# Expert stage: a large and a small expert share one pass, with their weight tiles in turn

## The chip, the cores and the metric

The kernel runs on one core of a Trainium2 chip. The metric is the device time of the program in microseconds (us), lower is better. Several runs of the kernel give a median; one further execution was recorded by the hardware profiler, and all rows below are from that one. Engines are named as in the profile: PE is the matmul engine (TensorE), PEld its weight loads, DVE is VectorE, ACT ScalarE, POOL GpSimd, SP the engine that issues the large loads.

## The reference, cut to what matters

A two-layer backbone in fp32 on 384 tokens (128 context, 256 latent). Layer 0 has an mLSTM and attention mixer and a dense SwiGLU, layer 1 a Mamba-2 mixer and then top-2-of-8 experts. The change touches the experts only, and the last residual and norm through what feeds them.

```python
D_MODEL = 1024; N_EXPERTS = 8; TOP_K = 2; D_FF_E = 1408

def swiglu(u, w1, w3, w2):
    return (jax.nn.silu(u @ w1) * (u @ w3)) @ w2

def moe_swiglu(u, router_w, router_b, w1, w3, w2):
    t = u.reshape(-1, d)                                  # 384 x 1024
    logits = (t @ router_w).astype(jnp.float32) + router_b.astype(jnp.float32)
    top_v, top_i = lax.top_k(logits, TOP_K)
    probs = jax.nn.softmax(top_v, axis=-1)
    gate = jnp.einsum('tk,tke->te', probs, jax.nn.one_hot(top_i, N_EXPERTS))
    for e in range(N_EXPERTS):
        out = out + gate[:, e:e + 1] * swiglu(t, w1[e], w3[e], w2[e])
```

## The kernel before

**Precision.** fp32 products are made of rounded parts. A weight tile (128 x 2816, 1408 KB) lands in one of four raw slots; ACT copies its high part into `whi` (`split`, L1235), DVE subtracts to get the low part `wlo` (`split`, L2247). There are three such pairs of buffers (`PAIRS = 3`), so ACT may split tile j only when PE has used tile j − 3 (`w_used`), and SP may load into a raw slot only when DVE has split what was in it (`split_lo`). `three` (L2934) makes hi·hi + hi·lo + lo·hi for 128 rows: three matmuls per block of 128 inputs. For 64 rows the high and the low part of the activations lie side by side in 128 columns ("packed"): two matmuls per block, with `whi` and `wlo`, and the two halves of the result's 128 lanes are then added (folded).

**Tiles.** An expert has 12 tiles: 8 up (tile 2f of `w1`, 2f + 1 of `w3`, 352 hidden columns each, f = 0 to 3) and 4 down (256 output columns each). A main up tile is 24 matmuls of 352 columns, a packed one 16; a main down tile is 33 matmuls of 256 columns, a packed one 22.

**Items.** The stage goes through a list of items; each is one pass over an expert's 12 tiles. Experts are ranked by their number of rows (expert 0 is apart and first). The three largest of the others have 128 main rows and 64 packed rows, the next has 128, the last three have 64. Rows beyond that go to further looped items.

| item | kind | what |
|---|---|---|
| 0 | main | expert 0; also ranks the experts and makes the item list |
| 1, 3, 5 | heavy (`heavy_item`) | ranks 0, 1, 2: 128 main and 64 packed rows on the same tiles |
| 2, 4 | light (`light_item`) | ranks 6, 5: 64 packed rows |
| 6 and on | main, in a hardware loop, at least one | rank 3, then rows left over |
| last | light, closing | rank 4: 64 packed rows |

**In an item.** PE takes the tiles in order; ACT applies silu from PSUM (L1275; packed L1311 copies the upper 64 lanes, L1316 is the silu), DVE makes the hidden product (`hidden`, L2413; packed `upper` L2431 and `packed_hidden` L2437 to L2439). After the last up tile PE transposes the hidden rows (`turn_h` L3366, `turn_packed` L3373), ACT and DVE split them, and the down tiles follow. Outputs are scaled by the gates when they leave PSUM (`out`, `packed_out` L1330 and L2454). ACT, DVE and POOL each have one queue in the program's order, so what waits holds back all behind it: `split` calls are written in between by hand.

**Rows of the next item.** DVE makes masks (`places`, `packed_places`), PE finds the row numbers with them (`find_rows` L3276, `packed_find` L3283), DVE turns them into indices (`next_rows`), POOL gathers the rows from `u_rows` in DRAM, PE transposes them in after the second down tile (`expert_in` L3292, `packed_in` L3299). POOL then adds the item's outputs to `y_rows` in DRAM (`scatter` L799, `packed_scatter` L808), each after the one before has landed (`y_added`). `rows_kept` (L2383) copies the indices for the scatter; in a looped item it waits for all scatters before.

**The end.** The closing item's outputs don't go through DRAM. POOL loads `y_rows` into `ytok` once the last scatter has landed, and `output_rows` (L3304, L3306) sums, for each of 8 blocks of 128 features, a matmul of `ye` with the one-hot `hotrow` (384 columns, two passes) and the transposed `ytok`. Four blocks go between the third and fourth down tile, four after it. The last residual and LayerNorm (`layer_norm`, `norm_steps`) follow.

Of the kernel before, what the change touches and what calls it, by code (L numbers as in the profile page):

```python
# [21 lines left out]
P = 128  # L22
# [24 lines left out]
ITEMS = NE + OVER  # L47
LAST = ITEMS - 1
# [3 lines left out]
Item = namedtuple("Item", "it m q h")  # L52
ITEM = (Item(0, 0, None, None), Item(1, 1, 0, 0), Item(2, None, 1, None), Item(3, 2, 2, 1), Item(4, None, 3, None),
        Item(5, 3, 4, 2))
LOOPED = len(ITEM)
RANKS = (0, 6, 1, 5, 2, 3, -1, -1, -1, -1, -1, 4)
ADDED = (0, 1, 4, 7)
PADDED = (2, 3, 5, 6, 8)


def looped(it):
    return Item(it, it - 2, None, None)


def closing(n):
    return Item(n, None, len(PADDED), None)


def next_main(x):

    if x.q == len(PADDED):
        return None
    if not isinstance(x.it, int) or x.it + 1 == LOOPED:
        return x.m + 1, x.it + 1
    return (ITEM[x.it + 1].m, x.it + 1) if ITEM[x.it + 1].m is not None else None


def next_packed(x):

    if not isinstance(x.it, int):  # L80
        return None
    if x.it + 1 == LOOPED:
        return len(PADDED), LAST, 0
    y = ITEM[x.it + 1]
    return (y.q, y.it, 0 if y.m is None else P) if y.q is not None else None


def added(m):
    return ADDED[m] if isinstance(m, int) and m < len(ADDED) else m + 5
# [7 lines left out]
for _n, _w in (("ident", 128), ("ropec", 128), ("ropes", 128),  # L97
               ("iota", 128), ("tri", 128), ("tie", 64), ("selp", 128), ("spread", 256), ("pm", 8), ("jrow", 16),
               ("erow", 8), ("rkrow", ITEMS - 1), ("caprow", 8), ("irow", OVER), ("tokc", 6), ("dummy", 2)):
    CI[_n] = (_at, _at + _w)  # L100
    _at += _w
# [40 lines left out]
def build(nc, i, o):  # L142
    ctx = ExitStack()
    with ctx:
# [243 lines left out]
        ye2 = rs.take(D, HALF)  # L388
# [6 lines left out]
        for _ in range(PAIRS):  # L395
# [4 lines left out]
        xp = rl.take(D).rearrange("p (k s) -> p k s", k=KB)  # L400
        heT2 = rl.take(FEB * P).rearrange("p (f s) -> p f s", f=FEB)
        rh = Region(arena[:, :], rl.at)
        he2, xrow2 = rh.take(FE, HALF), rh.take(D, HALF)
        fold2 = rh.take(2 * (FE // 4), HALF).rearrange("p (n w) -> p n w", n=2)
        part2 = he2[:, 0:D]
# [9 lines left out]
        ytok = [he[:, 0:D], spare[:, heT_at:heT_at + D], uT[:, :, :].rearrange("p a b -> p (a b)")[:, D:2 * D]]  # L415
        hotrow = he[:, D:D + T]
# [9 lines left out]
        gslot, gslot2 = re_.take(2), re_.take(3)  # L426
# [12 lines left out]
        hot, big2_ = (ro.take(OVER * 16) for _ in range(2))  # L439
        hotE, bigE = (ro.take((ITEMS - 1) * NE).rearrange("p (i e) -> p i e", i=ITEMS - 1) for _ in range(2))  # L440
        big = ro.take(C * (ITEMS - 1) * NE).rearrange("p (c i e) -> p c i e", c=C, i=ITEMS - 1)
        jover = ro.take(OVER)
        lists = sb("lists", [1, 16], I32)
        rows_in, rows_in2 = sb("rows_in", [P, 1], I32), sb("rows_in2", [P, 1], I32)
        rows_out, rows_out2 = sb("rows_out", [P, 1], I32), [sb(f"rows_out2_{n}", [P, 1], I32) for n in range(2)]
# [11 lines left out]
            "xp_lo": ("state_ready", 4), "packed_in_ready": ("num_ready", 2 * HA), "packed_out_ready": ("dspread_ready", 3),  # L457
# [56 lines left out]
        YBANK = (0, 1, 2, 3, 5, 0, 1, 2)  # L514
# [24 lines left out]

        def pbank(x, f, n):  # L540
            return ((5, 6), (4, 7))[f % 2][n] if x.h is not None else 2 * (f % 2) + n

        def obank(x, n):
            return (5, 6)[n] if x.h is not None else (7, 4)[n]
# [5 lines left out]
        def _(sp):  # L550
# [34 lines left out]
            def load_expert(e, s):  # L585
                sp.dma_start(slot(s % MRING), i["w_moe"][e, s] if isinstance(e, int) else
                             i["w_moe"][ds(e, 1), s].rearrange("a p n -> (a p) n")).then_inc(ready[s % MRING], 16)
# [3046 lines left out]
```

## Time and profile before

| | us |
|---|---|
| median of 3 runs | 1551.31 |
| lowest and highest run | 1545.7 and 1555.77 |
| profiled execution | 1554.25 |
| its span, first to last instruction | 1552.5 |
| PE busy in the span | 1418.6 |
| DVE busy | 1171.4 |
| ACT busy | 722.4 |
| expert stage to the end (996.8 to 1552.5) | 555.7 |

Busy time of PE counts each matmul from its start to its modelled end, and those overlap; the distance from one start to the next is what a matmul costs. Two engines can be busy at once, so busy times don't add up. Idle time of an engine matters only where PE or the end waits for it.

### The profile page before, as it was taken

The numbers are of one execution on the slowest core, as the hardware profiler recorded it, in microseconds if no ns is written. First come the engines' busy times: TensorE is split into PE (matmuls) and PEld (weight loads), VectorE is DVE, ScalarE is ACT, GpSimd is POOL, SyncE is SP. The second block draws the span as 40 slices with busy tenths as digits, with TensorE's granted clock in tenths as the row PEclk, the third lists the DMA queues.
The fourth block names the chain that finished last, engine by engine and source line by source line (L and its number), as shares of the span: only waits on it lengthen the run. The fifth ranks groups of instructions, "written<-read, shape, count | busy, mean of one in ns | idle before, by whom it ended". The sixth has DMA issues, their size and how long they took to land. (4 is left out here: it accounts for less than half of the span.)

```text
span 1552.5 us, 21728 instructions
## 1 busy us (share of the span) xinstructions
PE 1418.6 (91%) x8149; PEld 1273.2 (82%) x8149; DVE 1171.4 (75%) x1686; ACT 722.4 (47%) x1071; POOL 321.9 (21%) x409
## 2 busy tenths in 40 slices
PE   4999999799999997999999999889987997999966
PEld 1768876499999997998777698689987996999964
DVE  6868779768888796787778863787678659765885
ACT  1132223352333224644577742656466556656673
POOL 2201002720101003000699405300020001201103
PEclk9999999999999999999999899899999998999998
DMA  9525424445557541333322124478588759867871
GB/s 377 195 109 170 156 96 146 137 164 216 217 216 263 219 182 55 136 109 113 118 82 82 42 84 151 168 275 309 210 275 326 246 213 316 316 220 244 316 310 41
DMA packets 44718, 295.75 MB, mean 190 GB/s; under 512 B 5488, under 2 KB 5888, under 8 KB 21584
## 3 DMA queue, kind: packets, MB, share of 16 engines
q1 hardware_dynamic: 26496, 226.98, 39.7%
q0 software_dynamic: 17696, 65.94, 12.6%
q8 instruction: 60, 0.98, 0.3%
q10 hardware_dynamic: 432, 1.57, 0.3%
q14 instruction: 34, 0.28, 0.1%
HBM read 282.28 MB, written 12.19 MB: 190 GB/s over the span
## 5 line engine op out<-in xcount | busy, mean ns | idle before, releaser
L2247 DVE TENSOR_TENSOR arena_r<-arena,arena_r 128x2816 fp32r<-128x2816 f32 x96 | 295.2, 3086 | 95.1 <-ACT arena_r L1235 95.0
L1235 ACT ACTIVATE arena_r<-arena 128x2816 fp32r<-128x2816 f32 x96 | 244.9, 2553 | 92.1 <-PE ps L2937 68.8
L2937 PE MATMUL ps<-sqT_r,arena_r 128*128 128x384 f32 x963 | 261.0, 342 | 7.6 <-DVE uT_r L1896 7.6
L2937 PE MATMUL ps<-arena_r,uT_r 128*128 128x352 f32 (+2 forms) x636 | 204.5, 322 | 0.0
L2937 PEld LDWEIGHTS ps<-sqT_r,arena_r 128*128 128x128 f32 x963 | 178.4, 190 | 8.2 <-issue 8.2
L2937 PE MATMUL ps<-arena_r,zT_r 128*128 128x352 f32 x640 | 157.0, 328 | 7.1 <-DVE arena_r L2247 7.1
L2937 PE MATMUL ps<-arena_r,arena_r 128*128 128x384 f32 x848 | 159.9, 341 | 3.6 <-DVE zT L1907 2.4
L2937 PEld LDWEIGHTS ps<-arena_r,arena_r 128*128 128x128 f32 x848 | 150.0, 191 | 6.0 <-DVE zT L1907 2.7
L2937 PE MATMUL ps<-uT_r,arena_r 128*128 128x384 f32 x448 | 152.8, 341 | 0.0
L3334 PE MATMUL ps<-arena_r,arena_r 128*128 128x352 f32 x384 | 126.7, 332 | 17.1 <-DVE arena_r L2247 17.1
L3335 PE MATMUL ps<-arena_r,arena_r 128*128 128x352 f32 x384 | 124.5, 325 | 0.0
L2937 PEld LDWEIGHTS ps<-arena_r,uT_r 128*128 128x128 f32 x636 | 120.8, 190 | 4.4
L2937 PEld LDWEIGHTS ps<-arena_r,zT_r 128*128 128x128 f32 x640 | 113.1, 191 | 7.8 <-DVE arena_r L2247 7.7
L2700 PE MATMUL ps<-arena,uT 128*128 128x256 f32 x432 | 102.9, 393 | 0.3 <-DVE small L1762 0.3
L2700 PEld LDWEIGHTS ps<-arena,uT 128*128 128x128 f32 x432 | 82.4, 196 | 17.2 <-issue 5.5
L2937 PE MATMUL ps<-arena_r,spare_r 128*128 128x256 f32 (+1 forms) x504 | 96.1, 290 | 0.5 <-DVE arena_r L2247 0.5
L3334 PEld LDWEIGHTS ps<-arena_r,arena_r 128*128 128x128 f32 x384 | 73.5, 191 | 20.9 <-DVE arena_r L2247 19.6
L1881 DVE TENSOR_TENSOR arena_r<-arena,arena_r 128x2048 fp32r<-128x2048 f32 (+1 forms) x30 | 76.3, 2544 | 16.3 <-ACT arena_r L983 16.2
L2937 PEld LDWEIGHTS ps<-uT_r,arena_r 128*128 128x128 f32 x448 | 85.0, 190 | 0.0
L983 ACT ACTIVATE arena_r<-arena 128x2048 fp32r<-128x2048 f32 (+1 forms) x30 | 62.4, 2079 | 39.4 <-PE ps L2937 39.4
L2937 PEld LDWEIGHTS ps<-arena_r,spare_r 128*128 128x128 f32 x504 | 79.3, 189 | 1.0 <-DVE arena_r L2247 0.9
L3358 PE MATMUL ps<-arena_r,arena_r 128*128 128x256 f32 x264 | 70.9, 304 | 3.7 <-DVE arena_r L2445 3.6
(517 smaller groups left out, 2785.0 us busy)
## 6 DMA issues: line engine op xcount, KB each, us to landing
arena<-in_w_moe SPq DMA_DIRECT2D x96, 1408.0 KB, 6.5
arena<-in_w_up SPq DMA_DIRECT2D x22, 1024.0 KB, 5.8
zT<-in_w_adav POOLq DMA_DIRECT2D x32, 512.0 KB, 4.8
arena<-in_w_xbc SPq DMA_DIRECT2D x12, 1024.0 KB, 4.8
arena<-in_w_down SPq DMA_DIRECT2D x8, 1408.0 KB, 6.6
spare<-in_w_adav POOLq DMA_DIRECT2D x20, 512.0 KB, 5.2
sqT<-in_w_adav POOLq DMA_DIRECT2D x16, 512.0 KB, 3.7
arena<-in_w_z SPq DMA_DIRECT2D x8, 1024.0 KB, 4.8
```

The costliest lines, as they stand in the source:

```text
L983: nc.scalar.activation(fwhi[n % 2][:, 0:width], slot(g % RING)[:, 0:width], ACT.Copy) \
L1235: nc.scalar.activation(whi[s % PAIRS], slot(s % MRING), ACT.Copy) \
L1881: V.tensor_tensor(slot_r(g % RING)[:, 0:width], slot(g % RING)[:, 0:width], fwhi[n % 2][:, 0:width].bitcast(F32), ALU.subtract).then_inc(S ...
L2247: V.tensor_tensor(wlo[s % PAIRS], slot(s % MRING), whi[s % PAIRS].bitcast(F32), ALU.subtract) \
L2700: m = M.matmul(ps[:, bank + c, 0:256], uT[:, k, c * P:(c + 1) * P], slot(g % RING)[:, k * 256:(k + 1) * 256], start=k == 0, stop=k == KB - 1)
L2937: m = M.matmul(out, a, b, start=first and n == 0, stop=last and n == 2)
L3334: M.matmul(ps[:, pbank(x, f, n), 0:W], xp[:, k, :], whi[s % PAIRS][:, w], start=k == 0, stop=False)
L3335: e = M.matmul(ps[:, pbank(x, f, n), 0:W], xp[:, k, :], wlo[s % PAIRS][:, w], start=False, stop=k == KB - 1)
L3358: M.matmul(out, heT2[:, f, :], whi[s % PAIRS][:, w], start=f == 0, stop=False)
```

## The change

Heavy and light items disappear. A large expert and a small one now form a pair item of 24 tiles, one of each in turn (even tiles the large one, odd tiles the small one). Each even tile has 24 main and 16 packed matmuls, each odd one 16. The packed rows of both ("halves") share the 128 lanes of the folded values: the large expert's 64 rows in the lower lanes, the small one's in the upper. So there is one silu, one product and one set of transposes for both; the fold stays one per half and tile.

| item | kind | what |
|---|---|---|
| 0 | main | expert 0 |
| pair 0, 1 | pair | ranks 0 and 6, ranks 1 and 5 |
| looped, at least one | main | rank 3, then rows left over |
| closing pair | pair | ranks 2 and 4: 256 rows in the last pass |

Further: the halves' gate is multiplied into the hidden product, not onto the output. The main rows of a pair have PSUM banks 0 and 1 only (before 0 to 3). `xrow2`, the landing place of the next pair's gathered half rows, lies in `he2`, so its gather waits for the transposes of `he2`. POOL scatters the main rows, then half 0, then half 1, each after the one before has landed. `rows_kept` waits for main scatters only, and in a looped item it stands after split 6 instead of split 4. `ytok` lies in `xp` and a raw slot, so its loads wait until the closing pair has used its 16 up tiles and split 21 tiles (before: until the item ahead was done). `output_rows` has a second one-hot matmul, for the halves.

```diff
-ITEM = (Item(0, 0, None, None), Item(1, 1, 0, 0), Item(2, None, 1, None), Item(3, 2, 2, 1), Item(4, None, 3, None),
-        Item(5, 3, 4, 2))
-RANKS = (0, 6, 1, 5, 2, 3, -1, -1, -1, -1, -1, 4)
+PAIR_COLS = ((1, 2), (3, 4), (12, 13))
+ITEM = (Item(0, 0, None), Item(1, 1, 0), Item(3, 2, 1))
+RANKS = (0, 6, 1, 5, 3, -1, -1, -1, -1, -1, -1, 2, 4)
...
-        he2, xrow2 = rh.take(FE, HALF), rh.take(D, HALF)
+        he2 = Region(arena[:, :], rl.at).take(FE)
+        xrow2 = he2[:, 0:D]
...
+            def half_gather(h):
+                gp.wait_ge(*since("packed_in_ready", h + 1))
+                if h:
+                    gp.wait_ge(*since("phT_mm", h * 3))
...
-            gp.wait_ge(S("y_added"), n_last * 16 + 64)
-            gp.wait_ge(S("w_used"), n_last * MOE_TILES)
+            gp.wait_ge(S("y_added"), m_last * 16 + 16)
+            gp.wait_ge(*since("y_half", 64))
+            gp.wait_ge(S("split_lo"), n_last * MOE_TILES + 21)
+            gp.wait_ge(S("w_used"), n_last * MOE_TILES + 16)
...
+            def halves_hidden(x, f):
+
+                v.wait_ge(*since("psilu_ready", x.h * 4 + f + 1))
+                V.scalar_tensor_tensor(he2[:, f * (FE // 4):(f + 1) * (FE // 4)], fold2[:, 0, :],
+                                       gslot2[:, x.h:x.h + 1], fold2[:, 1, :], ALU.mult, ALU.mult) \
...
             def output_rows(b):
 
                 M.matmul(ps[:, YBANK[b], 0:T], ye[:, b * P:(b + 1) * P], hotrow, start=True, stop=False)
+                M.matmul(ps[:, YBANK[b], 0:T], ye2[:, b * P:(b + 1) * P], hotrow2, start=False, stop=False)
...
```

The three queues of a pair item, as the new code has them (ACT and DVE: first the first three groups of four tiles, then what follows; j is the tile):

```diff
+            def pair_item(x):                      # DVE
+                for f in range(3):
+                    fold(x, 0, f, 0)
+                    split(it, 4 * f + 3)
+                    fold(x, 1, f, 0)
+                    split(it, 4 * f + 4)
+                    hidden(x, f)
+                    fold(x, 0, f, 1)
+                    split(it, 4 * f + 5)
+                    fold(x, 1, f, 1)
+                    halves_hidden(x, f)
+                    split(it, 4 * f + 6)
+                    if f == 1:
+                        if last:
+                            rows_kept(x.m)
+                        else:
+                            next_rows(x)
...
+            def pair_item(x):                      # PE
+                for s in range(8):
+                    split_done(x, 2 * s)
+                    up_main(x, s, 2 * s)
+                    up_half(x, 0, s)
+                    split_done(x, 2 * s + 1)
+                    up_half(x, 1, s)
+                    if s == 1 and not last:
+                        next_found(x)
+                    elif s == 6:
+                        turn_h(x, 0, 2)
+                        turn_h(x, 1, 3)
+                turn_h(x, 2, 4)
+                turn_halves(x, 0, 2)
+                turn_halves(x, 1, 3)
+                for n in range(4):
+                    split_done(x, 16 + 2 * n)
+                    down_main(x, n, 16 + 2 * n)
+                    if n == 0:
+                        turn_halves(x, 2, 4)
+                    down_half(x, 0, n)
+                    if n == 1 and not last:
+                        halves_in(next_pair(x), (0, 3))
+                    elif n == 2 and not last:
+                        expert_in(next_main(x)[0], (0, 3))
+                    elif n == 2:
+                        for b in range(4):
+                            output_rows(b)
+                        first_mean(3)
+                    split_done(x, 17 + 2 * n)
+                    down_half(x, 1, n)
```

ACT in a group: `silu`, `lower(0)`, split 4f + 3, `lower(1)`, split 4f + 4, `halves_silu`, `lower(0)`, split 4f + 5, `lower(1)`, split 4f + 6. In the closing pair the last two folds of the outputs stand in DVE's queue behind the fourth block of the last residual.

## Rows read from the trace of the kernel before

**Rows 1.** Windows by item: stretch, its length, busy (count), PE clock, DMA share, GB/s

```profile
996.80:1057.70 60.90, 54.19 (x372) 52.83 (x371) 53.62 (x73) 37.36 (x25) 3.87 (x2) 0.97 0.79 291
1057.70:1194.20 136.50, 121.68 (x834) 118.94 (x832) 97.53 (x94) 82.22 (x71) 11.29 (x6) 0.96 0.76 270
1194.20:1329.80 135.60, 121.91 (x832) 119.17 (x832) 98.91 (x95) 80.84 (x70) 11.66 (x6) 0.96 0.76 271
1139.80:1194.20 54.40, 40.28 (x258) 38.27 (x256) 45.04 (x47) 39.80 (x33) 8.42 (x4) 0.91 0.90 319
1329.80:1413.50 83.70, 83.01 (x590) 82.24 (x591) 56.31 (x58) 42.33 (x39) 8.46 (x3) 1.00 0.67 239
1413.50:1470.00 56.50, 51.60 (x351) 50.83 (x350) 40.73 (x31) 35.69 (x23) 6.96 (x3) 0.97 0.82 305
1470.00:1524.50 54.50, 42.46 (x263) 38.60 (x261) 44.54 (x41) 33.91 (x30) 5.28 (x6) 0.94 0.65 252
1524.50:1552.50 28.00, 12.55 (x49) 8.19 (x48) 15.71 (x30) 10.47 (x19) 13.32 (x13) 0.79 0.15 56
1470.00:1498.40 28.40, 22.25 (x130) 20.26 (x128) 26.18 (x19) 22.07 (x18) 3.42 (x4) 1.00 1.00 381
```

Busy times stand in the order PE, PEld, DVE, ACT, POOL. The stretches are item 0, items 1 and 2, items 3 and 4, item 2 alone, item 5, the looped item, the closing item, the tail, and the up tiles of the closing item.

**Rows 2.** Order of time on PE, heavy items: start, us, what

```profile
1057.72 0.32 PE L3334 MATMUL ps<-arena_r,arena_r 128*128 128x352 f32 x1
...
1060.29 0.49 PE L2937 MATMUL ps<-arena_r,zT_r 128*128 128x352 f32 x2
...
1111.31 1.42 PE L3366 MATMUL ps<-cons,spare 128*128 128x128 f32 x11
...
1343.28 0.82 PE L3283 MATMUL ps<-spare,zT 128*128 128x16 f32 x6
```

**Rows 3.** Chain of waits in order of time, heavy item 3

```profile
1197.02 3.84 PE ps L2937 x24
...
1252.13 3.93 PE ps L2937 x33
```

**Rows 4.** Order of time on PE, light item 2, behind its last up tile

```profile
1175.72 1.44 PE L3373 MATMUL ps<-cons,arena 64*128 64x64 f32 x11 [5.47 <-DVE arena L2439]
```

**Rows 5.** Groups of heavy item 1 (busy us, mean ns, idle before), then of the stage

```profile
L2247 DVE TENSOR_TENSOR arena_r<-arena,arena_r 128x2816 fp32r<-128x2816 f32 x13 | 40.2, 3092 | 26.7 <-ACT arena_r L1235 26.7
L1235 ACT ACTIVATE arena_r<-arena 128x2816 fp32r<-128x2816 f32 x12 | 30.6, 2554 | 15.5 <-PE ps L2937 15.5
L1311 ACT ACTIVATE arena<-ps 64x352 f32<-64x352 f32 x8 | 3.7, 462 | 0.7 <-PE ps L3335 0.6
L2437 DVE TENSOR_TENSOR arena<-ps,arena 64x352 f32<-64x352 f32 x4 | 2.0, 511 | 0.0
...
L2454 DVE SCALAR_TENSOR_TENSOR sqT<-ps,spare,arena 64x512 f32<-64x512 f32 x10 | 7.4, 735 | 0.0
```

**Rows 6.** Chain of waits, looped item: the packed scatter of item 5

```profile
1422.53 11.18 DMA y_rows<-sqT,rows_out
```

**Rows 7.** Order of time on PE, looped item

```profile
1438.07 0.87 PE L2937 MATMUL ps<-arena_r,zT_r 128*128 128x352 f32 x2 [4.39 <-DVE arena_r L2247]
```

**Rows 8.** Order of time on PE, output blocks of the closing item

```profile
1515.81 0.81 PE L3304 MATMUL ps<-spare,sqT 128*128 128x384 f32 x2
1516.46 0.61 PE L3306 MATMUL ps<-cons,spare 128*128 128x128 f32 x4
...
1517.13 0.81 PE L3304 MATMUL ps<-spare,sqT 128*128 128x384 f32 x2
...
1526.99 1.65 PE L3304 MATMUL ps<-spare,sqT 128*128 128x384 f32 x2 [2.48 <-ACT sqT L1338]
```

**Rows 9.** DMA issues of the whole span: count, KB each, us to landing

```profile
arena<-in_w_moe SPq DMA_DIRECT2D x96, 1408.0 KB, 6.5
```

**Rows 10.** DMA issues from 1020 us on: count, us to landing

```profile
spare<-y_rows POOLq DMA_DIRECT2D x2, 512.0 KB, 11.7
...
arena<-u_rows,rows_in POOLq DMA_INDIRECT x6, 10.5
```

More of the change, by code:

```diff
@@ L1255, in rows_stored, with expert_in @@
                 act.dma_start(u_dram[c * P:(c + 1) * P, :], utok[:, c, :]).then_inc(S("u_stored"), 16)
-            def expert_in(m, halves=range(2), bank=0):
+            def expert_in(m, halves=range(2), banks=(0, 1)):
                 for n in halves:
@@ L1397, in light_item @@
[L1397 to L1412 removed]
+                    lower(x, 0, f, 0)
@@ new lines, in pair_item @@
+                split(it, 16)
+                halves_silu(x, 3)
+                lower(x, 0, 3, 1)
+                split(it, 17)
+                lower(x, 1, 3, 1)
+                hidden_hi(x, 2)
+                halves_hi(x, 0)
+                halves_hi(x, 1)
+                split(it, 18)
+                halves_hi(x, 2)
+                split(it, 19)
+                split(it, 20)
+                out(x, 0)
+                lower_out(x, 0, 0)
+                split(it, 21)
+                if not last:
+                    halves_in(next_pair(x), (0, 3))
@@ new lines, in next_rows, with output_slots @@
+                if next_pair(x) is not None:
+                    v.wait_ge(*since("found2_mm", next_pair(x) + 1))
+                slot_rows(*next_main(x))
+                if next_pair(x) is not None:
+                    half_rows(next_pair(x))
+            def inputs(x):
+                expert_in_lo(next_main(x)[0])
+                if next_pair(x) is not None:
+                    halves_in_lo(next_pair(x), (2, 3))
+            def output_slots(dst, row):
+                for c in range(C):
+                    step(V.tensor_scalar(rowc[:, c:c + 1], row, con("dummy")[:, 0:1], float(-P * c), ALU.add, ALU.add))
+                    V.tensor_scalar(dst[:, c * P:(c + 1) * P], con("iota"), rowc[:, c:c + 1], None,
+                                    ALU.is_equal).then_inc(S("hot_ready"), 1)
@@ L2506, in main_item @@
                 split(it, 6)
+                if not opening:
+                    next_rows(x)
                 split(it, 7)
@@ L3418, in main_item @@
                 for s in range(6):
+                    if s == 1 and not opening:
+                        pe.wait_ge(*since("ye2_ready", 2 * 4 - 1))
                     split_done(x, s)
-                    up_main(x, s)
+                    up_main(x, s, s)
                     if s == 0 and opening:
```

795 lines of the change are left out of this document (362 added, 433 removed).

## Prediction

> **What bounds the kernel now.** I read the windows by item first, then TensorE's order of time inside one heavy item, then the idle time in the light ones, then VectorE and ScalarE by group, and last the DMA. Only the expert stage is touched, 996.8 to 1552.5 us, so everything ahead of it is taken as unchanged.
>
> The windows [rows 1] show three kinds of item. A heavy item (a large expert's 128 rows plus 64 packed rows on the same weight tiles) keeps TensorE busy: item 5 has 83.0 busy of 83.7 us, at a granted clock of 1.00. A light item (64 packed rows alone) has TensorE busy 40.3 of 54.4 us, at 0.91. So the light items are held by something else, while the heavy ones are held by TensorE and leave VectorE and the DMA slack. A heavy-light couple takes 136.5 and 135.6 us.
>
> What TensorE needs follows from the starts of its matmuls [rows 2]. The 16 packed matmuls of a 352-column tile begin at 1057.72 and the next group at 1060.29: 2.57 us, 0.160 each. The chain of waits gives 3.84 for the 24 of the main rows and 3.93 for 33 of 256 columns [rows 3], so 22 packed ones of 256 columns take 2.62. Eleven 128-row transposes cost 1.4, one find of rows about 0.7 (0.82 less its overlap) [rows 2].
>
> In a light item an up tile is 2.57 us of TensorE, but VectorE needs 3.09 for its split (the low part of the weight tile) and 0.5 for each fold [rows 5], and at the turn from up to down nothing is left to multiply: TensorE waited 5.47 us for the last hidden product [rows 4]. The light item's clock of 0.91 [rows 1] adds to that.
>
> **The change, part by part.** Tiles stay 96 and the experts' row capacities stay (192 for the three largest, 128 for the next, 64 for three), so matmuls on weights stay equal in number. What changes is what stands beside what.
>
> *Pairs 0 and 1 take the place of two heavy-light couples.* TensorE per pair: up, 8 × (3.84 + 2 × 2.57) = 71.8; two finds 1.4; transposes of hidden values, 11 for the main rows and 11 for both halves together (before 11 + 11 + 11), 2.8; down, 4 × (3.93 + 2 × 2.62) = 36.7; 16 input transposes at 1.4/11 each, 2.0. Sum 114.7. Two of these are 229.4 against 272.1 [rows 1]: −42.7, if TensorE never waits.
>
> Does it wait? Take one group of four up tiles, 2 × (3.84 + 5.14) = 17.96 us of TensorE. VectorE has four splits (12.4), four folds (4 × 0.51), the main product (as a fold, 0.51) and one product for both halves (taken at 0.55 between 0.51 for the same columns and 0.74 for the 512-column scalar-tensor form, since it is now 352 columns with the gate as third operand): 15.5 [rows 5], or 86%. ScalarE has four splits at 2.55, four lower halves at 0.46 and two silus, taken at 0.5: 13.0 [rows 5]. A split of tile j+3 may begin when tile j is used (three split pairs). Counting from the group's start: tile 0 is used at 6.4; ScalarE copies the lower half (6.9), splits tile 3 (9.5), VectorE ends it at 12.6; it is wanted at 15.4. Tile 4 goes 12.5 on ScalarE and 16.2 on VectorE (a fold ahead of it); wanted at 17.96. The main product, now needed before the next main tile because the main rows have only banks 0 and 1, comes at 16.7: margin 1.3. Tiles 5 and 6 end at 21.5 and 25.6, wanted at 24.4 and 26.9. So every hand-off has 1.3 to 2.9 us. The next items' row numbers (some 2.2 us of one-column VectorE work, placed after the second group) eat one such margin.
>
> At the turn the transposes of blocks 0 to 7 of the main rows now lie between tiles 13 and 14, and the main down matmuls stand ahead of the halves' last transposes. The last hidden product of the halves comes about 2 us after tile 15, while TensorE has 1.4 us of transposes and 3.9 of main matmuls to do. The 5.47 wait has cover. Without it, it would come back at about 2 to 3 us a pair.
>
> The gate in the inner product removes the scaling at the output, where a scaled copy on ScalarE and a scaled add on VectorE (0.74 [rows 5]) become a plain copy and add. Outputs of halves double in number against items, not against experts: nothing, hidden under 9.2 us of TensorE per down step.
>
> *New waits.* The gather of the next pair's 128 half rows uses the space of the hidden values, so POOL may issue it only when the last halves' transposes are done, about 12 us before TensorE wants the rows. Gathers landed 10.5 us after issue in the median [rows 10]. Late, TensorE itself stands there with the next down tile behind it. I allow 0.75 in each of two pairs. Bounds 0 and 3. POOL now carries three scatters a pair, one after another, with a landing between (11.18 for one [rows 6]); the next gather of main rows is queued behind them. They end about 19 us into the next item and the rows are wanted at 40: nothing.
>
> *The looped main item.* Before, VectorE stood at the kept row numbers until a packed scatter had landed, at 1433.7 [rows 6]; the split behind it came late, and TensorE waited 4.39 [rows 7]. Now only the previous main scatter is awaited, and two splits later. TensorE needs 8 × 3.84 + 0.7 + 1.4 + 4 × 3.93 + 1.0 = 49.5 us and, at the turn, some 0.5 of waits, 50.0 against 56.5: −6.5.
>
> *Heavy item 5 and the closing light item become the closing pair.* Before 83.7 + 54.5 = 138.2. After: 114.7 less two finds and 16 input transposes = 111.3. Four output blocks lie inside it. One block took 1517.13 − 1515.81 = 1.32, of which the two-pass matmul on the rows is 0.65 (1516.46 − 1515.81) [rows 8]; a second such matmul makes 1.97, so 7.9, plus about 0.4 for the mean: 119.6. Difference −18.6. The three loads of the summed rows (11.7 us in the median [rows 10]) move from the item's start to after its split 21, some 10 us before the output blocks want them; before, weights shared the DMA, now three tiles are left. I allow 1.5, bounds 0 and 6.
>
> *The tail* keeps four output blocks: 4 × 0.65 = +2.6. The hand-off after the last weight matmul was 2.48 [rows 8], because ScalarE stood in squares; now a copy on ScalarE and an add on VectorE (0.74 at most) follow each other with the squares done: about 1.7. Net +1.8 on 28.0.
>
> *Item 0* has more one-column and small VectorE steps in the ranking and the places (three steps of about 0.2, three more place masks, four more row steps), on VectorE, which was busy 53.6 of 60.9 us there [rows 1]: +1.1.
>
> The sum: −42.7 − 6.5 − 18.6 + 1.8 + 1.1 = −64.9. Against it I put 1.5 for gathers, 1.5 for the loads and 4.5 for margins that don't hold in three pairs (1.5 each; 0 is the other bound, and twelve groups losing 1.5 each is the upper one, 18). That leaves −57.4. The profiled execution had 1554.25 us for a span of 1552.5, so 1496.9; the median of the runs is 2.9 lower, 1551.31, so **1494 us**.
>
> **A page against a row.** The matmuls of the expert stage start 0.160 us apart at 352 columns [rows 2, 3], at a clock of 1.00 in the heavy items [rows 1]. The Trainium skill (TensorE: Matmul & The Clock Gate, "Wait — 56ns, not 53.3ns?") gives columns over 2.4 GHz plus about 2.5 ns, here 149 ns. By that, the 448 up matmuls of a pair would be 4.8 us shorter, and three pairs would bring some 14 us more, an estimate from that page; but the row is of these very instructions and decides. The Trainium skill (DMA: Bandwidth & Descriptors, "Specifications") also sets some 358 GB/s as a core's limit from HBM, which would leave a pair's up phase only a tenth of reserve; in the closing item the trace has 381 GB/s over 28.4 us [rows 1], above that figure.
>
> **Rivals.** *A. The queues in order lose at the hand-offs.* A late fold or product holds back the split behind it. For it: margins of 1.3 us, and in the light item VectorE is exactly so chained. Against: in the heavy item VectorE idled 26.7 us in front of splits [rows 5] and TensorE did not notice. If two of each group's four tiles come 1 us late, that is 2 × 12 = 24 us: 1518.
>
> *B. Weights come late.* A pair's up phase wants two tiles of 1408 KB, 1.44 MB, [rows 9] in 8.98 us, 321 GB/s. Against: 381 at the closing item, with the DMA's share at 1.00 [rows 1], so that is about the top. For: only 270 over the couples, though those did not ask for more. If gathers, scatters and refills keep the 48 up tiles at 270 GB/s, each takes 5.34 instead of 4.49: +41, 1535.
>
> *C. Slower than before: the split ring serialises.* With three split pairs a tile may need the time between waits as VectorE shows it in the heavy item: 3.09 of work, 26.7/13 = 2.05 of idle before it [rows 5], and 0.77 of other work a tile, 5.9 us. Against 4.78 that TensorE needs, 72 tiles make +81: 1575. It decides against the change from 5.58 us a tile. Against it: that idle is VectorE waiting for ScalarE, which waits for TensorE, so it shrinks as TensorE becomes the one wanted sooner.
>
> *D. The change doesn't do what it says:* rows of this input overflow into one more item. Before, the loop ran once (96 tiles, eight items of twelve [rows 9]), and the capacities are the same; hardly possible.
>
> **Chances.** The forecast (1484 to 1506) 0.68; A 0.15; B 0.07; C with D 0.03; better than 1484, when no allowance is needed and the tail shrinks, 0.04; the rest 0.03 between B and the old time. The likeliest is the first. The range of 1484 to 1520 holds the first and A, and leaves out 0.17. A difference of about 1% (15 us) is what a measurement can tell from none: faster 0.93, same 0.04, slower 0.03.
>
> **What would show it.** Right: pairs of 115 to 117 us each with TensorE idle under 2 us and clock 1.00; main item about 51; closing pair about 121; tail 29 to 30; the DMA at about 300 GB/s over a pair. A shows as TensorE idle before an up tile, released by VectorE's split or product, in each group. B shows as ScalarE idle before its split, released by the weight DMA. A late gather shows as one TensorE idle after the second down tile; late loads as one before the first output block. The forecast is wrong if the splits' pace, not TensorE's matmuls, sets the time between tiles.

## The result, and the profile after

| | before | after |
|---|---|---|
| median of the runs, us | 1551.78 (4 runs) | 1491.38 (4 runs, 1490.29 to 1492.5) |
| span of the profiled execution | 1552.5 | 1488.6 |
| mean PE clock over the span | 0.965 | 0.973 |

The ratio of the times is 0.9614, with a 95% interval of 0.9581 to 0.9647. The forecast was 1494 with a range of 1484 to 1520.

The windows of the kernel after, by item (length, busy of PE, PEld, DVE, ACT, POOL, PE clock, DMA share, GB/s), answer to [rows 1]: item 0, pair 0, pair 1, the looped item, the closing pair, the tail.

```profile
996.80:1060.80 64.00, 57.89 (x376) 56.71 (x375) 55.87 (x82) 37.87 (x26) 3.91 (x2) 0.92 0.74 283
1060.80:1175.20 114.40, 114.34 (x809) 114.02 (x808) 95.95 (x82) 79.37 (x64) 6.84 (x4) 1.00 0.87 319
1175.20:1289.60 114.40, 114.35 (x809) 114.11 (x808) 97.53 (x82) 80.06 (x65) 13.17 (x5) 1.00 0.89 321
1289.60:1340.50 50.90, 50.09 (x351) 49.23 (x350) 44.68 (x32) 36.41 (x24) 5.91 (x3) 1.00 1.00 370
1340.50:1460.50 120.00, 119.95 (x822) 117.12 (x820) 96.54 (x83) 76.05 (x63) 13.75 (x13) 1.00 0.71 259
1460.50:1488.60 28.10, 13.64 (x58) 8.59 (x56) 13.86 (x25) 9.47 (x17) 4.84 (x5) 0.84 0.14 56
```

PE is busy 114.34 of the 114.40 us of a pair, at a granted clock of 1.00, where a heavy-light couple was 121.68 of 136.50 at 0.96. Of the 22.1 us that went, 14.8 are idle time of PE. The other 7.3 are busy time: shared transposes (some 1.4, an estimate from [rows 4]) and for the rest, as far as the rows tell, matmuls of the light item at a clock of 0.91.

What PE waited for in the kernel after from 1060 us to the end (us in total, times, longest):

```profile
PE ps L3325 <- DVE sqT L2470: 1.5, 1, 1.5
PE ps L3294 <- DVE zT L2288: 0.3, 1, 0.3
PE ps L3392 <- DVE spare L2429: 0.2, 1, 0.2
PE ps L2955 <- DVE arena_r L2254: 0.2, 1, 0.2
```

That is the whole list: the first is at the start of the tail, the others are in the looped item, and none lies inside a pair. The 5.47 before the packed transposes [rows 4] and the 4.39 of the looped item [rows 7] have gone. VectorE and ScalarE in pair 0, by groups (busy us, mean ns, idle before), beside [rows 5]:

```profile
L2254 DVE TENSOR_TENSOR arena_r<-arena,arena_r 128x2816 fp32r<-128x2816 f32 x24 | 74.1, 3089 | 12.8 <-ACT arena_r L1258 12.5
L2445 DVE TENSOR_TENSOR zT<-ps,zT 64x352 f32<-64x352 f32 x16 | 8.3, 518 | 2.4 <-ACT zT L1332 2.1
L2454 DVE SCALAR_TENSOR_TENSOR arena<-zT,spare 128x352 f32<-128x352 f32 x4 | 2.3, 584 | 0.1
...
L1258 ACT ACTIVATE arena_r<-arena 128x2816 fp32r<-128x2816 f32 x24 | 61.3, 2554 | 5.5 <-PE ps L3385 5.3
L1337 ACT ACTIVATE zT<-zT 128x352 f32<-128x352 f32 x4 | 2.0, 497 | 2.9 <-DVE zT L2445 2.9
```

The splits cost what they did (3089 and 2554 ns). VectorE's idle time before a split is 12.8 us over 24 of them, where a heavy item had 26.7 over 13. It was idle time that nobody needed.

### The profile page after: what moved, and what is told of

It is laid out like the page before. It is cut to its first block and busy times, and to the rows that moved or that the text cites. A ratio compares the mean times of both kernels' runs of the same rounds, so it can differ in the third digit from the quotient of the medians.

```text
span 1488.6 us, 21577 instructions
## 1 busy us (share of the span) xinstructions
PE 1399.9 (94%) x8076; PEld 1260.1 (85%) x8076; DVE 1172.0 (79%) x1654; ACT 719.1 (48%) x1054; POOL 308.9 (21%) x403
## 3 DMA queue, kind: packets, MB, share of 16 engines
q10 hardware_dynamic: 432, 1.57, 0.3%
## 5 line engine op out<-in xcount | busy, mean ns | idle before, releaser
L2254 DVE TENSOR_TENSOR arena_r<-arena,arena_r 128x2816 fp32r<-128x2816 f32 x96 | 295.7, 3088 | 43.6 <-ACT arena_r L1258 42.8
L2955 PEld LDWEIGHTS ps<-arena_r,arena_r 128*128 128x128 f32 x848 | 149.9, 191 | 6.3 <-DVE zT L1914 2.9
L3360 PE MATMUL ps<-arena_r,arena_r 128*128 128x352 f32 x384 | 123.1, 322 | 0.0
L3359 PE MATMUL ps<-arena_r,arena_r 128*128 128x352 f32 x384 | 122.9, 323 | 0.0
L3360 PEld LDWEIGHTS ps<-arena_r,arena_r 128*128 128x128 f32 x384 | 72.2, 188 | 0.0
L3359 PEld LDWEIGHTS ps<-arena_r,arena_r 128*128 128x128 f32 x384 | 72.0, 188 | 0.0
```

What stands on the lines that cost most here:

```text
L2254: V.tensor_tensor(wlo[s % PAIRS], slot(s % MRING), whi[s % PAIRS].bitcast(F32), ALU.subtract) \
L2955: m = M.matmul(out, a, b, start=first and n == 0, stop=last and n == 2)
L3359: M.matmul(ps[:, 2 + 2 * e + n, 0:W], xp[:, k, e, :], whi[j % PAIRS][:, w], start=k == 0, stop=False)
L3360: m = M.matmul(ps[:, 2 + 2 * e + n, 0:W], xp[:, k, e, :], wlo[j % PAIRS][:, w], start=False, stop=k == KB - 1)
```

## The experiments

Times are compared with the 1491.38 of the changed kernel unless another is named. Stages run from the first up tile of an item to that of the next. No experiment changes anything ahead of item 0, and yet item 0 starts between 994.3 and 998.5 us in the fourteen profiled executions. So a difference of 1 or 2 us between two medians of 4 or 5 runs says little, and where one matters the length of the stage in the trace is given beside it.

**1. One step of the looped item, alone in the kernel before.**

```diff
-                else:
-                    next_rows(x)          # looped item, after split 4
                 split(it, 5)
...
                 split(it, 6)
+                if not opening:
+                    next_rows(x)
                 split(it, 7)
```

> The kernel before, with one step of its looped item moved: VectorE's wait for the rows of the next item (next_rows) stands after the seventh split instead of the fifth. My theory of the 4.39 us for which PE stood in that item, and of the low clock behind it: VectorE waits there for a scatter to land, and every split behind it with it. Then 4.5 to 6 us go (1546 to 1547.3). The rival: the looped item is bound by its loads (16 DMA engines busy for 1.00 of the time around the stall) and PE waits for weights instead: 0 to 2 us off.

Measured: 1545.14 against 1551.02 of the kernel before on the same chip, ratio 0.9961 (0.9947 to 0.9975). The window of the looped item, where [rows 1] had 56.50 at clock 0.97:

```profile
1409.80:1460.20 50.40, 49.90 (x352) 49.41 (x350) 40.85 (x31) 35.70 (x23) 6.39 (x3) 1.00 0.92 342
```

Theory holds: 5.9 us. PE has no idle time over 0.25 us there. Of the change's 60 us these 6 don't need the pairs at all.

The same trace has a second lesson. Its light items, whose code is that of before, took 51.1 and 51.3 us where the profile of before had 54.4 and 53.4. This is the first of them, and PE's wait there for the last hidden product:

```profile
1141.50:1192.55 51.05, 39.49 (x258) 37.53 (x256) 44.85 (x47) 39.79 (x33) 8.24 (x4) 0.93 0.94 338
```

```profile
1174.69 0.90 PE L3373 MATMUL ps<-cons,arena 64*128 64x64 f32 x11 [2.74 <-DVE arena L2439]
```

The 5.47 of [rows 4] is one execution's number, and some 5 us of what the two pairs save differ between these two executions.

**2. The same step put back in the changed kernel.**

```diff
+                else:
+                    v.wait_ge(*since("y_half", 64))
+                    next_rows(x)          # looped item, after split 4
...
-                if not opening:
-                    next_rows(x)          # after split 6
```

> The changed kernel, with the same step of the looped item put back where it was before the change, after the fifth split, and waiting for the scatters of both pairs' small halves. My theory: the half scatter of pair 1 is issued at 1312.2 us and lands 11 us later, so that VectorE stands from about 1301 to 1323, the splits behind it with it, and PE for 15 to 20 us: 1506 to 1516. The rival: the transfers of the item are its bound (50.9 us with DMA at 1.00), and the wait only moves what they would cost: under 3 us longer.

Measured: 1502.32, 10.9 us longer, between the two. First VectorE's wait at the kept row numbers, then the idle time of PE that it makes, then the windows of that idle time and of the stretch behind it:

```profile
1316.54 0.15 DVE L2402 COPY rows_out<-rows_in 128x1 int32<-128x1 int32 x1 [11.85 <-DMA y_rows<-sqT,rows]
```

```profile
1320.79 0.95 PE L2956 MATMUL ps<-arena_r,zT_r 128*128 128x352 f32 x2 [10.06 <-DVE arena_r L2254]
```

```profile
1310.00:1320.80 10.80, 0.74 (x6) 0.45 (x4) 3.95 (x8) 2.90 (x2) 3.54 (x2) 0.78 0.44 135
1320.80:1330.00 9.20, 9.20 (x43) 9.18 (x44) 6.89 (x4) 2.58 (x2) 0.80 (x1) 0.70 0.89 350
```

The item takes 63.8 instead of 51.0 us. The mechanism is right and two sizes were off. The last scatter, issued at 1311.4, had landed by 1316.5 and not 11 us later, so VectorE stood from 1304.7 to 1316.5. And PE had split tiles in hand until 1310.7. The rest of the 12.8 us is the clock, 0.70 behind the stall.

**3. Two 64-lane instructions in place of each shared one.**

```diff
-                nc.scalar.activation(fold2[:, 0, :], fold2[:, 0, :], ACT.Silu)
+                nc.scalar.activation(fold2[lanes64(0), 0, :], fold2[lanes64(0), 0, :], ACT.Silu)
+                nc.scalar.activation(fold2[lanes64(1), 0, :], fold2[lanes64(1), 0, :], ACT.Silu)
...                                         # and the gated product in the same way
```

> The two products that the halves of the small expert share over 128 lanes (the Silu on ScalarE, the gated product on VectorE) are each made as two instructions of 64 lanes: 12 more on either engine. My theory: both engines have about 2.4 us of slack in each group of 17.96 us, the extra 0.5 to 0.6 us an instruction is hidden, and the time stays within 1 us of the changed kernel (1491 +- 1); at the last group, where the small expert's hidden tiles feed the down tiles, no more than 0.3 us a pair. The rival: the hand-offs between ring, lower and fold are tight (1.3 us), and an instruction more on each engine shows as a wait of PE in each group: 12 times 0.5 = 6 us longer.

Measured: 1495.22, 3.8 us longer; ratio to before 0.9640 (0.9627 to 0.9653), so neither theory. PE's idle times in pair 0, which pair 1 and the closing pair repeat in part:

```profile
1117.08 0.56 PE L2957 MATMUL ps<-arena_r,zT_r 128*128 128x352 f32 x2 [0.68 <-DVE spare L2430]
...
1144.30 0.38 PE L3386 MATMUL ps<-arena_r,zT_r 128*128 128x256 f32 x1 [0.78 <-DVE zT_r L2463]
```

It isn't hidden and isn't lost in every group. It shows at two places: at the last group of four tiles (0.68 in pair 0, 0.43 in pair 1), behind which VectorE had also made the next items' row numbers, and at the first packed down tile (0.78 in each of three pairs), where what comes late is the low part of the transposed hidden values. The closing pair, which makes no row numbers, has no wait at its last group. The waits add up to 3.4 us, and sharing lanes is worth the 3.8 that the runs show.

**4. VectorE's margins, measured with work added.** Reductions that nobody reads stand ahead of `hidden` in VectorE's queue: two of 352 columns in three groups of each pair, then four of 1024 (1210 ns each in the trace) in two groups.

```diff
                     split(it, 4 * f + 4)
+                    for r in range(4 if f < 2 else 0):       # or: range(2), 352 columns
+                        k = (x.h * 2 + f) * 4 + r
+                        V.tensor_reduce(filler[:, k:k + 1], cons[:, 0:1024], X, ALU.add)
                     hidden(x, f)
```

> Two reductions of 128x352 on VectorE (about 0.52 us each, by a 128x312 reduction's 0.478) are added ahead of the gated product in three of the four groups of each pair: 9 groups, 9.4 us of VectorE in all; their outputs are read by nobody. My theory: 1.04 us fits into the 2.4 us that a group leaves VectorE and into hand-offs of 1.3 us or more: within 1 us of the changed kernel. The rival (the queues in order lose at hand-offs as soon as VectorE comes later): 9 times 0.5 to 1.0 = 4.5 to 9 us longer.

Measured: 1491.30, no change in the median. In the trace the pairs took 115.2 and 115.0 us instead of 114.4, and from item 0 to the end it is 493.6 instead of 491.4, which an item 0 that started 1.4 us earlier hides in the total. PE has two new idle times:

```profile
1115.51 0.56 PE L2959 MATMUL ps<-arena_r,zT_r 128*128 128x352 f32 x2 [0.66 <-DVE spare L2430]
...
1230.52 0.56 PE L2959 MATMUL ps<-arena_r,zT_r 128*128 128x352 f32 x2 [0.43 <-DVE spare L2430]
```

Both are at the last group of a pair, where experiment 3 had them. With about 1.04 us added, 0.66 and 0.43 came through: some 0.4 and 0.6 us were left there, and over 1.04 in the other groups that had work added.

> Four reductions of 128x1024 on VectorE (about 1.22 us each) are added ahead of the gated product in the first two groups of each pair: 6 groups, 29 us of VectorE in all. My theory: VectorE has 2.46 us of slack in a group of 17.96, so 4.9 exceeds it by 2.4 us in each of 6 groups; two groups together 4.8 us, of which the lead that the ring and the later groups give takes back 1 to 2.5: 2.5 to 4 us a pair, 8 to 12 us in all. The rival: the slack is far larger than worked out (VectorE's waits hide it), and the time moves by less than 3 us.

Measured: 1520.18, 28.8 us longer, far above both theories. PE's idle times in pair 0, and a window behind the first:

```profile
1083.05 0.56 PE L2959 MATMUL ps<-arena_r,zT_r 128*128 128x352 f32 x2 [2.16 <-DVE spare L2430]
1106.20 0.93 PE L2959 MATMUL ps<-arena_r,zT_r 128*128 128x352 f32 x2 [3.39 <-DVE spare L2430]
```

```profile
1083.00:1106.00 23.00, 19.76 (x112) 19.50 (x112) 19.75 (x15) 12.64 (x11) 0.00 (x0) 0.90 0.68 248
```

The first says that 4.84 − 2.16 = 2.7 us were free in the first group. The sum of six such waits is 17.7 us; the pairs grew by 9.9, 8.9 and 10.7, together 29.5. So 12 of the 29 us are not waiting but, as far as the trace tells, matmuls at a lower clock, 0.90 between the stalls. The expectation worked from VectorE's share of a group's time. What counts is how late one product is, and what each stall then does to the clock.

**5. The order of the tiles.** Two tiles of the large expert, then two of the small one, with all queues in that order.

```diff
-                f, n, j = s // 2, s % 2, 2 * s + e
+                f, n, j = s // 2, s % 2, 4 * (s // 2) + 2 * e + s % 2
...                                         # loads, splits, lowers and folds follow
```

> The same pass of a pair, but the up tiles of a group run in the order A A B B (two of the large expert, then two of the small one) instead of in turn; loads, splits, lowers and folds follow in the same order, and every instruction is still there. My theory: the ring holds three split pairs and two large tiles in a row leave 5.14 us of matmuls, less than the lower, split and split that must come back before the next large tile can start (5.7 to 6.6 us), so each of the 12 groups loses 1 to 1.5 us and the kernel takes 12 to 18 us longer than the changed kernel (1503 to 1510 us). The rival: only the sum of work on VectorE and ScalarE over a group counts (15.5 of 17.96 us), and the order of tiles doesn't matter: 1490 to 1493 us, with PE never idle inside a pair.

Measured: 1502.41, 11.0 us longer. PE's idle times in pair 0:

```profile
1096.56 0.59 PE L2958 MATMUL ps<-arena_r,zT_r 128*128 128x352 f32 x2 [1.01 <-DVE arena_r L2257]
1115.79 0.60 PE L2958 MATMUL ps<-arena_r,zT_r 128*128 128x352 f32 x2 [1.01 <-DVE arena_r L2257]
1140.46 0.50 PE L2958 MATMUL ps<-arena_r,spare_r 128*128 128x256 f32 x2 [1.53 <-DVE uT_r L2440]
1142.36 0.39 PE L3387 MATMUL ps<-arena_r,arena_r 128*128 128x256 f32 x1 [0.18 <-DVE arena_r L2464]
```

The mechanism holds, the size doesn't: 11.0 us is below the 12 to 18 of the theory, and 7 of the 12 groups lose time, not all. It is 1.01 in the third and the fourth group of pairs 0 and 1 and 1.09 in the last three of the closing one, 7.3 us in all. The rival, that only the load counts, is out, since the load is the same. Another 5.1 us, which the theory did not have, are the turn to the down tiles (1.53 and 0.18 in each pair), where the low part of the main rows' hidden values now comes late. The clock stayed at 1.00 behind waits of 1.0 us, as behind the first of them:

```profile
1096.50:1100.50 4.00, 3.94 (x24) 3.94 (x25) 3.91 (x4) 3.35 (x3) 0.00 (x0) 1.00 0.74 248
```

**6. The gates, back at the output.**

```diff
-                V.scalar_tensor_tensor(he2[...], fold2[:, 0, :], gslot2[:, x.h:x.h + 1], fold2[:, 1, :], ALU.mult, ALU.mult)
+                V.tensor_tensor(he2[...], fold2[:, 0, :], fold2[:, 1, :], ALU.mult)
...                                         # and scale=gslot2 in the output's copy and add
```

> The gate part of the change alone is undone: the halves' hidden product is a plain product, and the gate is applied at the output again (a scaled copy on ScalarE, a scaled add on VectorE). My theory: this part was worth nothing; in the pairs both are hidden under TensorE, and at the end of the last pair the scaled add takes at most 0.06 us more than the plain one (0.735 before against 0.688 after), twice: within 0.5 us of the changed kernel in its span, 1490 to 1493 us by the runs. The rival: the output's hand-offs are tight, and 12 scaled copies and 12 scaled adds cost 0.1 us each on the path: 2 to 3 us longer.

Measured: 1489.37 (1489.08 to 1493.35), pairs of 114.3 us. Item 0 starts 1.8 us earlier in this trace, and from there to the end it takes 492.1 us, where the changed kernel takes 491.4. This part is worth nothing that can be measured.

**7. More weight traffic.** Copies of a tile from HBM to HBM in SP's queue: 2, 6 and 12 in each pair.

```diff
                     load_expert(e[j % 2], j // 2, j)
+                    if j in (2, 5, 8, 11, 14, 17):
+                        sp.dma_start(spare_dram[...], i["w_moe"][h, j // 3]).then_inc(S("copied"), 16)
```

> Each pair gets 2 more transfers in the weights' own queue: copies of one weight tile (1408 KB) from HBM to a part of HBM that nobody reads. It asks how near the weights were to being late (rival B of the prediction). My theory: at 370 to 381 GB/s a copy takes the 16 DMA engines 3.8 us; a pair leaves them 0.11 to 0.13 of 114.4 us free, 12 to 15 us, so 2 copies (7.6 us) fit, apart from a short wait where one stands in front of a weight tile: 0 to 3 us longer in all. The rival: the reserve is used up at once, since a copy both reads and writes: each of the 6 copies costs 3.8 us or more, 23 us and up.

Measured: 1491.57, no change.

> The same with 6 copies in each pair. My theory: 6 times 3.8 is 22.8 us against 12 to 15 us free, so a pair grows by 8 to 11 us, and the kernel by 24 to 33 us (1515 to 1524), with PE idle ahead of up tiles, released in the end by the weights' DMA. The rival (a copy costs its reading and its writing, 7.6 us): 46 against 12 to 15 free, 31 to 34 us a pair, about 95 in all.

Measured: 1493.23, 1.9 us longer, far below both theories. Windows of pair 0's first 71 us in the changed kernel and then in this one, and what ScalarE waited for there, between 1060 and 1461 us:

```profile
1060.80:1132.00 71.20, 71.20 (x452) 71.10 (x451) 61.20 (x60) 49.32 (x40) 2.77 (x2) 1.00 0.90 326
```

```profile
1060.80:1132.00 71.20, 71.20 (x452) 71.09 (x451) 61.82 (x60) 49.05 (x41) 1.67 (x2) 1.00 1.01 415
```

```profile
ACT arena_r L1262 <- DMA arena<-in_w_moe: 20.5, 18, 3.0
```

A DMA share of 0.90 did not mean that a tenth was left. With a quarter more bytes PE is still busy for all of the 71.2 us. ScalarE waits for weights 18 times, and most of that is taken up by the time it would have waited for PE. Not all: pair 1 took 115.7 us instead of 114.4, with PE waiting 0.22 and 0.61 us in it.

> Twelve copies of a tile (1408 KB) from HBM to HBM in each pair's weight queue, after six a pair had cost only some 2 us at 415 GB/s in the up phase. It looks for the rate at which the weights do come late. By bytes a pair moves 36.5 MB and 17.3 more: at 114.4 us that is 470 GB/s. If 415 to 427 GB/s is near the top of the engines (they were busy for 1.00 of the time there), a pair needs 126 to 130 us: 12 to 16 more, 35 to 48 us in all. The rival (the rate goes on rising with demand): under 10 us in all.

Measured: 1534.13, 42.8 us longer, as expected by bytes. Windows of pair 0 and of pair 1, then ScalarE's wait for weights between 1060 and 1460 us:

```profile
1058.10:1182.80 124.70, 117.35 (x809) 115.65 (x807) 95.71 (x82) 79.29 (x64) 6.71 (x4) 0.99 1.01 421
1182.80:1312.20 129.40, 119.12 (x807) 117.17 (x807) 97.99 (x83) 79.59 (x65) 10.02 (x6) 0.97 1.01 419
```

```profile
ACT arena_r L1262 <- DMA arena<-in_w_moe: 119.4, 42, 5.8
```

So about 420 GB/s is what the DMA gave here, and the pairs of the change ask for 320, and 326 in their up tiles. Of the 42.8 us, 8.61 are one wait of PE for `y_rows`, whose loads landed in 12.2 us (median) where they had landed in 6.8. The expectation by bytes did not have that wait, so it is partly luck that the total lies in its range.

**8. Item 0's search, later.**

```diff
-                    elif s == (4 if opening else 1):
+                    elif s == (5 if opening else 1):
                         outputs_read(x)
                         next_found(x)
```

> Item 0's search for the rows of the next items (TensorE's part) stands after its sixth up tile instead of its fifth, that is two tiles' matmuls, 5 us, later than the point where VectorE has its table ready; nothing else changes. My theory: the 2.10 us that PE waits for VectorE there go, and with them the fall of the clock around them (0.67 of full speed over 10 us, where it was 0.83 before the change): 2 to 4 us off the changed kernel, 1487.4 to 1489.4. The rival: the gather of the pair's packed rows starts 2.5 us later and lands too late for its transposes, and PE waits at the start of pair 0 instead: 0 to +2 us.

Measured: 1485.88 (1484.86 to 1487.75), ratio 0.9583 (0.9564 to 0.9602); each of its runs is below the lowest of the changed kernel, though the two intervals of the ratio overlap a little. Item 0 takes 59.7 us instead of 63.6. That is 5.5 us in the median, more than the 2 to 4 expected. In the profiles the whole difference is 5.7 us, but 2.05 of them lie ahead of item 0, where nothing differs. The 9.1 us behind the find in the changed kernel, and the same stretch counted from the start of item 0 in this one:

```profile
1024.90:1034.00 9.10, 9.08 (x41) 9.01 (x42) 7.17 (x9) 1.19 (x2) 0.00 (x0) 0.62 0.77 297
```

```profile
1022.80:1031.90 9.10, 8.91 (x61) 8.67 (x60) 8.86 (x20) 4.03 (x4) 0.00 (x0) 1.00 0.80 303
```

The idle time didn't go. In the changed kernel PE's waits in item 0 are 3.52, 2.10, 0.25 and 0.24, 6.1 us; here they are 3.43, 1.50, 0.19, 1.30 and 0.25, 6.7. What went is the low clock: 0.62 became 1.00, and the same 9.1 us hold 61 matmul records instead of 41. So the 3.9 us of item 0 are the clock's, and the expectation, which counted the idle time too, had it half wrong.

It is the clock behind the find that counts, not the one ahead of it. The changed kernel's clock was low ahead of it as well, behind the wait of 3.52 us. Ten traces leave item 0 as it is, and in five of them (experiments 2, 3 and 6, the first of 4 and the second of 7) the clock stayed at 1.00 there. Below are the first 4 us behind that wait in the changed kernel, the same 4 us in the first run of experiment 4, and PE's wait for the find in that run:

```profile
1017.15:1021.15 4.00, 4.00 (x18) 4.00 (x19) 3.72 (x9) 0.00 (x0) 0.00 (x0) 0.69 0.76 270
```

```profile
1015.74:1019.74 4.00, 4.00 (x24) 3.84 (x24) 3.72 (x9) 0.00 (x0) 0.00 (x0) 1.00 0.76 251
```

```profile
1023.50 0.81 PE L3298 MATMUL ps<-spare,zT 128*128 128x16 f32 x6 [3.63 <-DVE zT L2289]
```

PE comes to the find 1.5 us sooner, waits 3.63 instead of 2.10, and the find begins 27.7 us into the item in both, when VectorE's table is ready. Item 0 takes 63.6 us either way. In two more of the ten traces (experiment 5 and the third of 7) the clock behind the find was 0.81 instead of 0.62 over 9.1 us, and item 0 took 62.2 and 62.1.

**9. The half masks later too.** On top of experiment 8, VectorE makes the six half masks after its third product, PE finds the half rows after the second turn, and `next_rows` stands after split 8.

> The version with the later find (e5_find_later), and in addition the packed half of item 0's search moved on: VectorE's six half masks stand after its third hidden product, TensorE's half find after the transposes of tiles 0 to 7, and the row numbers after the eighth split. My theory: item 0 is held by VectorE, and taking 1.5 us of masks (6 of 0.25) and the half row steps from ahead of the splits takes the 1.30 us that PE waits at its second block of transposes, while the gathers, issued some 3 us later, still land in time: 0.5 to 1.5 us below the 1485.9 of the later find. The rival: the gathers land too late for the input transposes, or VectorE only waits elsewhere: 0 to 3 us above it.

Measured: 1490.49, 4.6 us above experiment 8. One wait on PE, and the head of what VectorE did ahead of the product that ended it:

```profile
1037.70 0.90 PE L3394 MATMUL ps<-cons,spare 128*128 128x128 f32 x3 [3.24 <-DVE spare L2429]
```

```profile
1034.55 0.17 DVE L2369 COPY spare<-ps 128x16 f32<-128x16 f32 x1 [1.57 <-issue]
...
1037.13 0.52 DVE L2429 TENSOR_TENSOR spare<-ps,spare 128x352 f32<-128x352 f32 x1
```

The masks and row steps still stand ahead of VectorE's last hidden product, so no work was taken from it, and 1.57 us of waiting came on top, for which the profile names no releaser; PE's half find, 1033.72 to 1034.46, ends just ahead of the copy that reads it. The product ends the wait at 1037.1 instead of 1035.9, PE waits 3.24 instead of 1.30, and the clock behind is lower:

```profile
1040.00:1050.00 10.00, 10.00 (x74) 10.00 (x74) 8.22 (x3) 5.35 (x5) 0.00 (x0) 0.82 0.82 318
```

Item 0 is back at 63.3 us, and the median is above both theories. The best version is experiment 8's.

## Why the prediction was right, step by step

| term | forecast, us | measured, us |
|---|---|---|
| two pairs | 229.4 | 228.8 |
| looped item | 50.0 | 50.9 |
| closing pair | 119.6 | 120.0 |
| tail | 29.8 | 28.1 |
| item 0 | 62.0 | 63.6 |
| allowances | 7.5 | 0 |

**The sum of PE's instructions** carried the forecast, and it was exact: 114.7 a pair against 114.4, and in the closing pair 119.6 against 120.0. Distances between starts in the trace of before, counted out over the new order, gave each of these stages and the looped item to 0.9 us, since PE really became the bound.

**The allowances** were not needed, 0 of 7.5 us. The gathers of half rows landed in 9.5 us (median) with PE never waiting. The loads of `y_rows` landed in 6.8 us instead of the 11.7 of [rows 10], issued at 1431.3 and wanted at 1440.1: in the profiled execution of the changed kernel that held exactly. In nine of the eleven traces of its versions PE waited 0.2 to 0.8 us for them (0.8 in experiment 4, 0.3 in 8), so the 0 of this term is in part luck. The hand-offs, for which 4.5 was set aside, had 2.7 us in the first group by experiment 4, where the forecast had worked out 1.3 for the main product, but only 0.4 to 0.6 at the last one, behind the row numbers. The forecast said that these would eat one margin, and they nearly did.

**Item 0** was undersized, 2.7 us more than before instead of 1.1. The added VectorE steps are as costed: the find begins 27.7 us into the item instead of 26.8. What the term left out is the clock behind the find, 0.62 over 9.1 us where it was 0.81 before. In experiment 5's trace, with 0.81 there, the item is 1.4 us shorter, and with 1.00 in experiment 8 it is 3.9 shorter with VectorE's work unchanged.

**The tail** was oversized, +0.1 instead of +1.8, in the term "4 × 0.65". It added 0.65 a block to the tail as it was, and that tail held a slow block. Before, the first block behind PE's wait took 2.72 us to the next (1526.99 to 1529.71), at a low clock (0.51):

```profile
1526.90:1530.00 3.10, 3.01 (x9) 2.41 (x10) 0.32 (x2) 0.56 (x2) 3.02 (x3) 0.51 0.00 0
```

Now it runs at about the pace of the others, 1.96, where the forecast had 1.97:

```profile
1462.17 0.88 PE L3325 MATMUL ps<-spare,sqT 128*128 128x384 f32 x2 [1.50 <-DVE sqT L2470]
1464.20 0.81 PE L3325 MATMUL ps<-spare,sqT 128*128 128x384 f32 x2
```

That block takes 2.03, with its second matmul; four take 7.9 against 7.0. The hand-off is 1.50 where 1.7 was forecast.

**From the sum to the median.** 555.7 less 491.4 is 64 us in the spans. The median moved by 60.4, because the profiled execution of before lay 2.5 us above its median and that of after 0.9 below. So part of the closeness is luck. In the traces the forecast of the stage is 6.9 us too long (498.3 against 491.4), and the allowances alone are 7.5. It had taken off 2.9 us on the ground that the profile would lie above the median again; it lay below, and that took the miss down to 2.6.

**The rivals.** A (losses at hand-offs) did not happen, but it is near: experiment 5 brings it about with the same instructions in another order, 11.0 us, and experiment 3 with one more instruction on either engine, 3.8 us. B (weights late) was further away than the forecast thought: its step "so that is about the top", at 381 GB/s, is refuted by 415 in experiment 7. C took the VectorE idle time of the heavy item for a cost of the ring; it fell to a quarter, from 2.05 to 0.53 us a split, as the text against it said. D did not occur.

Still open: why PE waits up to 0.8 us for the `y_rows` loads in most traces and not in that of the changed kernel, since their median landing differs by 0.1 us at most between it (6.8) and that of the two small reductions in experiment 4 (6.9), where the wait was 0.76. Open too is why the clock ahead of the find in item 0 is low in some executions and not in others, and how much of the change's gain belongs to the order of tiles as opposed to the pairing itself. The light items could not be given another cover without the pairing, so this was not tried.

## What to carry to other kernels

Where one kind of pass leaves PE idle and another leaves the helpers idle, put their tiles in turn and count the matmuls' distances from start to start: if PE then bounds, the count is the time. Check the hand-offs one by one in the order of each queue, not by the share of busy time, and give the tiles in turn, large and small: with three buffers, taking them two and two cost 11 us here. Look at the clock behind a wait of PE before pricing it by its length. Six waits of 2.2 to 3.4 us, 17.7 in all, cost 29.5 us in experiment 4; in item 0 the low clock behind the find cost 3.9 us, while the low clock ahead of it cost nothing, because PE then waited for VectorE anyway.

## What the hardware showed that was not expected

- **Reserve of the DMA.** A share of 0.90 at 326 GB/s went to 1.01 at 415 GB/s with PE undisturbed over 71.2 us, and about 420 was the ceiling. The share of busy time did not grow in step with the bytes, so the room left was more than 1 less the share. The Trainium skill (DMA: Bandwidth & Descriptors, "Specifications") sets some 358 GB/s from HBM for a core; 415 over 71.2 us is 16% above it, and the measurement decides. The same page calls 358 GB/s the share of each of two cores that stream at once, and has 425 GB/s as measured on one core alone; the 419 to 421 of experiment 7, on one core, agree with that.
- **The clock after a wait.** It stayed at 1.00 behind waits of 1.0 us (experiment 5), and was 0.90 between waits of 2.2 and 3.4 us (experiment 4) and 0.70 behind one of 10.06 us (experiment 2). It is not the same each time. In all twelve traces of the changed kernel and its versions PE waits 3.4 to 3.5 us at the same place of item 0, with the same instructions up to there; over the 4 us behind it the clock was 1.00 in six of them and 0.57 to 0.70 in the other six.
